# Modulation vectors of a transformer stack: one PSUM bank per group of weight slots, rows copied and turned once per group

## The chip, the cores and the metric

One Trainium2 chip, one core of it. The metric is the device time of one launch in microseconds; the kernel before took 2061.79 us (median of 3 runs, 2061.45 to 2061.92).

## The reference, cut to what matters

The kernel computes two blocks of two layers each, on 256 context tokens and 256 latent tokens of width 1024, later 16 + 256 tokens. The change concerns the modulation of the first block alone. For each of its two layers one vector for the latent tokens and one for the context tokens is made from a condition vector, and cut into six parts of 1024 numbers each (shift, scale and gate, twice):

```python
mod_lat = (silu_c @ ada_w[i] + ada_b[i])[:, None, :]
mod_ctx = (silu_cc @ ada_w[i] + ada_b[i])[None, None, :]
sh1, sc1, g1, sh2, sc2, g2 = jnp.split(mod_lat, 6, axis=-1)
...
h_lat = modulate(rmsnorm(x, norm_g[i, 0]), sh1, sc1)
...
x = x + g1 * rmsnorm(y_lat, norm_g[i, 1])
h = modulate(rmsnorm(x, norm_g[i, 2]), sh2, sc2)
x = x + g2 * rmsnorm(conv_ffn(h, ...), norm_g[i, 3])
```

`ada_w[i]` is 1024 by 6144, so both layers hold 48 pieces ("slots") of 1024 by 256, 1 MB each. The two vectors (latent and context) are multiplied together, as two columns of one small operand.

## The kernel before, in words

**Streams.** All activations lie with features on the 128 partitions. Every projection streams its weights in slots of 1 MB: SyncE loads `w_raw`, ScalarE writes `w_hi` (the rounded part), VectorE `w_lo` (the rest), and TensorE makes three products for each (lines 456 to 458, or 451 to 453). A projection of width 512 tokens has 16 steps (j) to a slot of 48 matmuls. The order of all work on an engine is the order in which the program is written; engines wait for each other by semaphores. A `fill` or `after` function puts other work between the steps or slots of a projection.

**The modulation.** A slot's product (`pe_ada_products`, matmuls on line 570) is written as rows: the stationary operand is `cvec[:, k, :]`, 32 columns of which two hold the condition vectors and 30 are zero, and the moving operand is a block of 256 columns of the slot. The eight k are spread over four groups of 32 partitions of the bank `wk[:, 2]`, two k in each, so the result is four partial sums of two rows by 256. ScalarE copies them to `ada_rows` (line 580), and two matmuls on line 593 (`pe_ada_columns`) turn them into columns and add the four parts at the same time: `ada_rows` is the stationary operand (128 by 128), and two columns of `pad` with ones in the rows 32 q and 32 q + 1 are the moving one. The result is written to `wk[:, 3]`, from which VectorE takes whole parts (`dve_mod`, line 641).

**Where the slots stand.** Eight slots are in the opening, in four pairs on two banks (`pe_ada_first`). The other 40 (g = 0 to 39) come through a ring of two buffers, `ada_ring`; ScalarE issues the load of slot g + 2 behind the copy of slot g (line 583). Slots 0 to 5 stand between the steps of the first projections, 6 to 11 in `hyb_out`, 12 to 20 around the first residual (`pe_residual`, lines 990 and 993) and the second norm (`pe_norm`, line 730: squares are summed over partitions, and slots 16, 17 and 18 stand behind the chunks c = 1, 3 and 5), 21 to 30 in the first half of the feed-forward layer, and 31 to 39 around the second residual and the third norm, as 12 to 20. In these two stretches ScalarE squares X (line 743), takes the roots (lines 999 and 747) and writes the modulated values (line 757), and VectorE takes the reciprocals (lines 1005 and 765) and updates X (line 1011). In what follows they are called the first and the second norm stretch.

**Waits.** TensorE's products of slot g wait for the ring's load of g and for ScalarE's copy of slot g - 1, because both use one bank. Its columns of slot g - 1 stand behind the products of slot g. ScalarE's copy of slot g waits for the columns of slot g - 1, because there is one buffer for the rows, and so does everything behind it on ScalarE, the load of slot g + 2 too.

## Time and profile before

| | |
|---|---|
| median of 3 runs | 2061.79 us (2061.45 to 2061.92) |
| span of the profiled execution | 2060.0 us, core clock 0.979 on average |
| own time of the profiled execution | not given apart; the runs lie 1.5 to 1.9 us above its span |
| TensorE matmul busy | 1965.3 us (95%) |
| VectorE, ScalarE, GpSimd busy | 1250.8, 934.2 and 217.6 us |
| TensorE's share of the chain that ended last | 85% |
| data moved | 296.79 MB, 144 GB/s on average |

The span is the time from the first to the last instruction of one profiled execution. Busy shares say how long an engine had work in hand; the chain that ended last says which work the end had to wait for. PEclk in a table of windows is the granted clock of TensorE as a share of 2.4 GHz.

### The profile page before, as it was taken

How to read it: one execution, taken by the hardware profiler on the slowest of the kernel's cores; microseconds unless marked ns; L12 is line 12 of the kernel's file. 1: busy time of each engine (PE TensorE's matmuls, PEld its weight loads, DVE VectorE, ACT ScalarE, POOL GpSimd, SP SyncE). 2: the span in 40 equal slices, each digit the busy share in tenths (PEclk: the TensorE clock that was granted, in tenths of full speed). 3: DMA queues.
4: the chain of work that ended last, by engine and by line, in shares of the span. 5: the costliest groups of instructions: out<-in, count | busy, mean ns of one | idle time of the engine just before them, and what ended most of it. 6: DMA issues, size and time to landing. Idle time of an engine off the chain costs nothing.

```text
span 2060.0 us, 33586 instructions
## 1 busy us (share of the span) xinstructions
PE 1965.3 (95%) x13381; PEld 1743.3 (85%) x13381; DVE 1250.8 (61%) x1853; ACT 934.2 (45%) x1477; POOL 217.6 (11%) x171
## 2 busy tenths in 40 slices
PE   5999989999999899999989998999999999989998
PEld 3776647778888579999979997998899999879997
DVE  5354455543555445667577677656975557787564
ACT  4344335332333343148455455346654444565353
POOL 2100103440452000012000000000010010000001
PEclk8999989999999999999989999999999999999999
DMA  8621464433222523222435543542345554224553
GB/s 351 221 82 62 146 243 143 164 132 118 88 89 85 204 82 123 83 103 83 143 130 172 188 166 130 184 164 79 127 164 177 171 177 143 101 90 167 186 182 123
DMA packets 43952, 296.79 MB, mean 144 GB/s; under 512 B 4976, under 2 KB 6128, under 8 KB 11696
## 3 DMA queue, kind: packets, MB, share of 16 engines
q1 hardware_dynamic: 36576, 247.48, 34.8%
q10 hardware_dynamic: 6048, 42.49, 5.9%
q0 software_dynamic: 1200, 5.02, 0.7%
q8 instruction: 91, 1.49, 0.3%
q14 instruction: 37, 0.30, 0.0%
HBM read 293.93 MB, written 1.05 MB: 143 GB/s over the span
## 4 chain that ended last, share of the span: by engine, by line
PE 85%; DVE 7%; ACT 4%; DMA 2%; issue 1%; POOL 1%; SPq 0%; ACTq 0%; DVEq 0%; POOLq 0%
PE acc L456 23%; PE acc L458 22%; PE acc L457 22%; PE acc L451 2%; PE acc L452 2%; PE acc L453 2%; DVE w_lo L393 2%; PE wk L570 2%; DMA ada_first<-in_w_ada 1%; PE wk L1671 1%; PE wk L730 1%; ACT w_hi L383 1%; PE wk L593 1%; PE acc L1660 1%; PE wk L1400 1%
## 5 line engine op out<-in xcount | busy, mean ns | idle before, releaser
L456 PE MATMUL acc<-Hhi,w_hi 128*128 128x272 f32 (+2 forms) x2304 | 742.2, 322 | 26.0 <-DVE Hlo L772 9.1
L458 PE MATMUL acc<-Hhi,w_lo 128*128 128x272 f32 (+2 forms) x2304 | 719.7, 312 | 0.0
L457 PE MATMUL acc<-Hlo,w_hi 128*128 128x272 f32 (+2 forms) x2304 | 718.9, 312 | 0.0
L393 DVE TENSOR_TENSOR w_lo<-w_raw,w_hi 128x1024 fp32r<-128x1024 f32 (+2 forms) x472 | 572.1, 1251 | 181.5 <-ACT w_hi L383 179.9
L383 ACT ACTIVATE w_hi<-w_raw 128x1024 fp32r<-128x1024 f32 (+2 forms) x472 | 452.5, 1005 | 434.0 <-PE acc L458 348.1
L456 PEld LDWEIGHTS acc<-Hhi,w_hi 128*128 128x128 f32 x2304 | 439.8, 191 | 68.9 <-issue 36.0
L457 PEld LDWEIGHTS acc<-Hlo,w_hi 128*128 128x128 f32 x2304 | 440.0, 191 | 21.8
L458 PEld LDWEIGHTS acc<-Hhi,w_lo 128*128 128x128 f32 x2304 | 439.4, 191 | 22.4
L456 PE MATMUL acc<-Fhi,w_hi 128*128 128x256 f32 (+2 forms) x864 | 264.8, 307 | 2.6 <-DVE w_lo L393 1.5
L458 PE MATMUL acc<-Fhi,w_lo 128*128 128x256 f32 (+2 forms) x864 | 264.4, 306 | 0.0
L457 PE MATMUL acc<-Flo,w_hi 128*128 128x256 f32 (+2 forms) x864 | 264.1, 306 | 0.0
L456 PEld LDWEIGHTS acc<-Fhi,w_hi 128*128 128x128 f32 x864 | 163.4, 189 | 11.2 <-issue 2.2
L458 PEld LDWEIGHTS acc<-Fhi,w_lo 128*128 128x128 f32 x864 | 163.4, 189 | 7.0
L457 PEld LDWEIGHTS acc<-Flo,w_hi 128*128 128x128 f32 x864 | 163.1, 189 | 6.7
L451 PE MATMUL acc<-w_hi,Hhi 128*128 128x256 f32 x320 | 93.2, 291 | 0.0
L1046 ACT ACTIVATE cgu<-acc,vec 128x512 f32<-128x512 f32 x44 | 34.2, 779 | 127.1 <-PE acc L458 127.1
L452 PE MATMUL acc<-w_lo,Hhi 128*128 128x256 f32 x320 | 90.4, 283 | 0.0
L453 PE MATMUL acc<-w_hi,Hlo 128*128 128x256 f32 x320 | 90.4, 283 | 0.0
L1068 DVE SCALAR_TENSOR_TENSOR cgu<-acc,vec,cgu 128x510 f32<-128x510 f32 x44 | 32.7, 745 | 92.0 <-ACT cgu L1046 92.0
L957 DVE COPY Y<-acc 128x256 f32 (+3 forms) x32 | 17.9, 558 | 81.0 <-PE acc L458 81.0
L1905 DVE TENSOR_TENSOR X<-acc,X 128x272 f32<-128x272 f32 (+3 forms) x48 | 20.4, 434 | 73.6 <-PE acc L458 73.6
L451 PEld LDWEIGHTS acc<-w_hi,Hhi 128*128 128x128 f32 x320 | 61.2, 191 | 3.2 <-issue 3.0
(390 smaller groups left out, 2452.4 us busy)
## 6 DMA issues: line engine op xcount, KB each, us to landing
w_raw<-in_w_ffn_in SPq DMA_DIRECT2D x44, 1024.0 KB, 4.9
ada_ring<-in_w_ada ACTq DMA_DIRECT2D x40, 1024.0 KB, 4.9
w_raw<-in_w_mlp_in SPq DMA_DIRECT2D x32, 1024.0 KB, 4.9
w_raw<-in_w_mlp_out SPq DMA_DIRECT2D x32, 1024.0 KB, 4.9
w_raw<-in_w_ffn_out SPq DMA_DIRECT2D x32, 704.0 KB, 4.1
ada_first<-in_w_ada SPq DMA_DIRECT2D x8, 1024.0 KB, 17.9
w_raw<-in_w_ret_v SPq DMA_DIRECT2D x8, 1024.0 KB, 4.8
w_raw<-in_w_ret_g SPq DMA_DIRECT2D x8, 1024.0 KB, 4.9
```

The costliest lines, as they stand in the source:

```text
L383: act.activation(w_hi[:, r, a:b], w_raw[:, r, a:b], ACT.Copy).then_inc(hi_done, 1)
L393: dve.tensor_tensor(w_lo[:, r, a:b], w_raw[:, r, a:b], w_hi[:, r, a:b].bitcast(F32), ALU.subtract).then_inc(lo_done, 1)
L451: pe.matmul(o, x_hi(k)[:, toks], w_hi[:, r, w], start=k == 0, stop=False)
L452: pe.matmul(o, x_hi(k)[:, toks], w_lo[:, r, w], start=False, stop=False)
L453: mm = pe.matmul(o, x_lo(k)[:, toks], w_hi[:, r, w], start=False, stop=k == last)
L456: pe.matmul(o, w_hi[:, r, w], x_hi(k), start=k == 0, stop=False)
L457: pe.matmul(o, w_hi[:, r, w], x_lo(k), start=False, stop=False)
L458: mm = pe.matmul(o, w_lo[:, r, w], x_hi(k), start=False, stop=k == last)
L570: mm = pe.matmul(wk[b:b + 32, ada_bank(s), 0:256], cvec[:, k, :], w[:, k * 256:(k + 1) * 256], start=k < 4, stop=k >= 4)
L593: mm = pe.matmul(wk[:, 3, 2 * m:2 * m + 2], ada_rows_of(s)[:, c * P:(c + 1) * P], V("pad", 0, 2), start=True, stop=True)
L1046: act.activation(cgu[:, r, c, 0:n], acc_tile(p, r, c), ACT.Identity, bias=Vd("conv_b", m + layer * 44), scale=Vd("conv_w", m + (layer * 3 ...
L1068: dve.scalar_tensor_tensor(seqs(o, 1, SEQ), seqs(acc_tile(p, r, c), 0, SEQ - 1), w, seqs(o, 1, SEQ), ALU.mult, ALU.add).then_inc(conv_left, 1)
```

## The change

Nine groups of slots take the place of 48 single ones: the four pairs of the opening, and the slots 0 to 5, 6 to 11, 12 to 20, 21 to 30 and 31 to 39 of the ring.

- The slots of a group accumulate in one bank. Slot j of a group uses a window of the stationary operand `cvec` that is shifted by 2 j columns, so its two rows land in the rows 2 j and 2 j + 1 of each 32, and all other rows get zero added. `cvec` is now 62 columns wide, and the condition vectors stand in columns 30 and 31.
- Only the first slot of a group waits for a copy (of the group before). ScalarE copies once for each group, with the last slot; for the others it only waits for the products and issues the load of slot g + 2.
- The rows are turned once for each group (`pe_ada_close`, two matmuls with 2 w moving columns for w slots, from `pad`, which now holds four identities of 32 by 32). A close is added in the feed-forward layer, behind its slot 0, for the group 12 to 20.
- `cvec` takes the memory of `rope_c`, so `rope_c` is loaded later, in `load_second` on GpSimd's queue, and the late constants are nine loads in place of ten. VectorE's memset of `cvec` has 496 elements a partition in place of 256, and `vec` has 27 columns more.

```diff
-        ("lru_lam", 8), ("subln", 1), ("lambda", 256), ("if_bias", 2), ("eps", 1), ("pad", 5),
+        ("lru_lam", 8), ("subln", 1), ("lambda", 256), ("if_bias", 2), ("eps", 1), ("pad", 32),
...
+        cvec = at("cvec", [P, DC, 62], at_const[0])
         rope_c = const("rope_c", [P, 2, T2])
...
-        ADA_READ = {ADA_LATE: 8, 0: 4, ADA_HYB: 5, ADA_OUT: 6}
+        ADA_GROUPS = [(0, ADA_HYB, 4), (ADA_HYB, ADA_OUT, 5), (ADA_OUT, ADA_FFN, 6), (ADA_FFN, ADA_LATE, 6), (ADA_LATE, ADA_RING, 8)]
+        ADA_PAIRS = ADA_FIRST // 2
...
-            if ada_back(s) > 0:
-                pe.wait_ge(ada_staged, ada_back(s))
+        def ada_products(pe, w, j, bank, first, last):
+
             for k in range(DC):
                 b = 32 * (k % 4)
-                mm = pe.matmul(wk[b:b + 32, ada_bank(s), 0:256], cvec[:, k, :], w[:, k * 256:(k + 1) * 256],
-                               start=k < 4, stop=k >= 4)
+                mm = pe.matmul(wk[b:b + 32, bank, 0:256], cvec[:, k, 30 - 2 * j:62 - 2 * j], w[:, k * 256:(k + 1) * 256],
+                               start=first and k < 4, stop=last and k >= 4)
             mm.then_inc(ada_used, 1)
 
+        def act_ada_pair(act, i):
+            act.wait_ge(ada_used, 2 * i + 2)
+            if i >= 2:
+                act.wait_ge(ada_done, i - 1)
+            act.activation(ada_rows[0][:, i % 2, :], wk[:, 1 + i % 2, 0:256], ACT.Copy).then_inc(ada_staged, 1)
+
         def act_ada(act, first, last):
 
             for s in range(first, last):
+                n, a, b, _ = ada_group(s - ADA_FIRST)
                 act.wait_ge(ada_used, s + 1)
-                if ada_back(s) > 0:
-                    act.wait_ge(ada_done, ada_back(s))
-                act.activation(ada_rows_of(s), wk[:, ada_bank(s), 0:256], ACT.Copy).then_inc(ada_staged, 1)
-                if ADA_FIRST <= s < 2 * ADA_SLOTS - 2:
+                if s - ADA_FIRST == b - 1:
+                    if n >= 1:
+                        act.wait_ge(ada_done, ADA_PAIRS + n)
+                    act.activation(ada_rows[1][:, 0, :], wk[:, 2, 0:256], ACT.Copy).then_inc(ada_staged, 1)
+                if s < 2 * ADA_SLOTS - 2:
                     g = s + 2 - ADA_FIRST
                     act.dma_start(ada_ring[:, g % 2, :], t["w_ada"][s + 2]).then_inc(ada_ring_loaded[g % 2], 16)
...
+        def pe_ada(pe, g):
+
+            n, a, b, _ = ada_group(g)
+            pe.wait_ge(ada_ring_loaded[g % 2], 16 * (g // 2 + 1))
+            if g == ADA_HYB:
+                pe.wait_ge(at_pt, 32)
+            if g == a:
+                pe.wait_ge(ada_staged, ADA_PAIRS + n)
+            ada_products(pe, ada_ring[:, g % 2, :], g - a, 2, g == a, g == b - 1)
+
+        def pe_ada_close(pe, g):
+
+            n, a, b, read = ada_group(g - 1)
+            pe.wait_ge(ada_staged, ADA_PAIRS + n + 1)
+            pe.wait_ge(s_mod, read)
+            x, w = 4 * (ADA_FIRST + a), b - a
             for c in range(2):
-                m = 2 * ada_slot(s) + c
-                mm = pe.matmul(wk[:, 3, 2 * m:2 * m + 2], ada_rows_of(s)[:, c * P:(c + 1) * P], V("pad", 0, 2),
+                o = wk[:, 3, x:x + 4 * w].rearrange("p (j x) -> p j x", x=4)[:, :, 2 * c:2 * c + 2]
+                mm = pe.matmul(o, ada_rows[1][:, 0, c * P:(c + 1) * P], V("pad", 0, 2 * w).rearrange("p (j s) -> p j s", s=2),
                                start=True, stop=True)
             mm.then_inc(ada_done, 1)
...
-            act_ada(act, 6, 8)
+            act_ada_pair(act, 3)
             hi(2)
             hi(3)
...
+            pool.dma_start(rope_c[:, :, :], t["rope_c"]).then_inc(s_meta, 16)
...
             def slots(s):
+                if s == 0:
+                    pe_ada_close(pe, ADA_FFN)
                 if ADA_FFN + s < ADA_LATE:
                     pe_ada(pe, ADA_FFN + s)
```

**TensorE in the feed-forward layer.** Between two slots of the projection, TensorE had a slot's products (line 570) and the columns of the slot before (line 593):

```order
L458 MATMUL acc<-Hhi_66,w_lo 128x512
L570 MATMUL wk<-ada_ring,cvec 32x256 x8
L593 MATMUL wk<-vec,ada_rows_89 128x2 x2
L456 MATMUL acc<-Hhi_66,w_hi 128x512
L457 MATMUL acc<-Hlo_69,w_hi 128x512
```

In the changed kernel the same place (products are now line 550) reads:

```order
L458 MATMUL acc<-Hhi_67,w_lo 128x512
L550 MATMUL wk<-ada_ring,cvec 32x256 x8
L456 MATMUL acc<-Hhi_67,w_hi 128x512
L457 MATMUL acc<-Hlo_70,w_hi 128x512
L458 MATMUL acc<-Hhi_67,w_lo 128x512
```

The two matmuls on `ada_rows` have gone; the products stand where they stood.

**TensorE at the start of the first norm stretch.** Before, from the last step of `hyb_out` over slots 12 and 13, the residual's sums (990, 993), slots 14 and 15, to the first two chunks of the norm (730):

```order
L458 MATMUL acc<-SGhi,w_lo 128x512
L570 MATMUL wk<-ada_ring,cvec 32x256 x16
L593 MATMUL wk<-vec,ada_rows_89 128x2 x2
L990 MATMUL wk<-sq_acc,ones 128x512
L993 MATMUL wk<-sq,ones 128x512 x2
L570 MATMUL wk<-ada_ring,cvec 32x256 x8
L593 MATMUL wk<-vec,ada_rows_89 128x2 x2
L570 MATMUL wk<-ada_ring,cvec 32x256 x8
L593 MATMUL wk<-vec,ada_rows_89 128x2 x2
L730 MATMUL wk<-sq,ones 128x512 x2
```

And now (the residual's sums are lines 991 and 994):

```order
L458 MATMUL acc<-SGhi,w_lo 128x512
L550 MATMUL wk<-ada_ring,cvec 32x256 x16
L991 MATMUL wk<-sq_acc,ones 128x512
L994 MATMUL wk<-sq,ones 128x512 x2
L550 MATMUL wk<-ada_ring,cvec 32x256 x16
L730 MATMUL wk<-sq,ones 128x512 x2
L550 MATMUL wk<-ada_ring,cvec 32x256 x8
```

Three pairs of column matmuls between `hyb_out` and the norm have gone, and nothing has come in; behind each later pair of norm chunks one more is gone.

**ScalarE at the end of the first norm stretch.** Before, from the last two squares to the first modulated value (line 757); line 580 is the copy of a slot, line 583 the ring's load:

```order
L743 ACTIVATE sq<-X 128x512 x2
L580 ACTIVATE ada_rows_89<-wk 128x256
L583 DMA ada_ring<-in_w_ada 128x2048
L747 ACTIVATE root<-wk,vec 128x512
L580 ACTIVATE ada_rows_89<-wk 128x256
L583 DMA ada_ring<-in_w_ada 128x2048
L580 ACTIVATE ada_rows_89<-wk 128x256
L583 DMA ada_ring<-in_w_ada 128x2048
L757 ACTIVATE n_78<-nt,mod,gains 128x256 x2
```

And now (the copy of a group is line 568, the ring's load line 571):

```order
L743 ACTIVATE sq<-X 128x512 x2
L571 DMA ada_ring<-in_w_ada 128x2048
L747 ACTIVATE root<-wk,vec 128x512
L571 DMA ada_ring<-in_w_ada 128x2048
L568 ACTIVATE ada_rows_90<-wk 128x256
L571 DMA ada_ring<-in_w_ada 128x2048
L757 ACTIVATE n_79<-nt,mod,gains 128x256 x2
```

Two of the three copies have gone, with their waits for TensorE's columns; one stays, that of the whole group with slot 20, ahead of the first modulated value.

## Rows read from the trace of the kernel before

**Rows 1.** The page's part 4: shares of the chain that ended last.

```profile
PE 85%; DVE 7%; ACT 4%; DMA 2%; issue 1%; POOL 1%; SPq 0%; ACTq 0%; DVEq 0%; POOLq 0%
```

**Rows 2.** Busy us by stretch, summed over 46:108, 220:271 and 308:460.

```profile
sum 265.00, PE 264.11 PEld 205.45 DVE 126.20 ACT 98.73 POOL 80.77; mean PE 88.04 PEld 68.48 DVE 42.07 ACT 32.91 POOL 26.92
```

**Rows 3.** One source line, L593: duration ns min/median/max, first and last start.

```profile
L593 PE MATMUL wk<-vec,ada_rows x192: 165/251/374, 22.4 to 724.1; 128*128 128x2 f32 x192
```

**Rows 4.** Timeline, TensorE, 226 to 236: start us, us, engine, line, idle before.

```profile
226.78 0.39 PE L458 MATMUL acc<-SGhi,w_lo 128*128 128x512 f32 x1
227.09 1.07 PE L570 MATMUL wk<-ada_ring,cvec 128*32 128x256 f32 x16
...
228.91 0.40 PE L456 MATMUL acc<-AThi,w_hi 128*128 128x512 f32 x1
...
232.80 0.39 PE L458 MATMUL acc<-SGhi,w_lo 128*128 128x512 f32 x1
...
234.12 0.61 PE L593 MATMUL wk<-vec,ada_rows 128*128 128x2 f32 x4
...
235.37 0.39 PE L456 MATMUL acc<-SGhi,w_hi 128*128 128x512 f32 x1
```

**Rows 5.** The chain in order of time, 272 to 306: start us, us, what.

```profile
273.28 0.28 ACT ada_rows L580
...
274.77 0.54 PE wk L593 x4
...
276.27 1.73 PE wk L993 x4
...
278.03 0.70 ACT root L999
...
289.99 1.82 PE wk L730 x4
...
296.83 4.80 DMA ada_ring<-in_w_ada
...
305.10 1.10 ACT n L757 x2
```

**Rows 6.** Timeline, 273 to 303: start us, us, engine, line, idle before.

```profile
273.70 1.07 PE L570 MATMUL wk<-ada_ring,cvec 128*32 128x256 f32 x16 [1.33 <-ACT ada_rows L580]
...
302.68 1.29 DVE L777 TENSOR_TENSOR nt<-X,rstd 128x512 f32<-128x512 f32 x2
```

**Rows 7.** Timeline, 690 to 724: start us, us, engine, line, idle before it.

```profile
690.13 1.07 PE L570 MATMUL wk<-ada_ring,cvec 128*32 128x256 f32 x16 [0.81 <-ACT ada_rows L580]
...
694.45 0.69 ACT L999 ACTIVATE root<-wk,vec 128x512 f32<-128x512 f32 x1 [0.94 <-PE wk L993]
...
698.90 1.94 PE L570 MATMUL wk<-ada_ring,cvec 128*32 128x256 f32 x16 [2.95 <-DMA ada_ring<-in_w_ada]
...
699.84 0.88 DVE L1011 SCALAR_TENSOR_TENSOR X<-nt,gains,X 128x256 f32<-128x256 f32 x2
...
701.36 0.87 DVE L1011 SCALAR_TENSOR_TENSOR X<-nt,gains,X 128x256 f32<-128x256 f32 x2
...
701.88 0.38 ACT L580 ACTIVATE ada_rows<-wk 128x256 f32<-128x256 f32 x1 [5.45 <-PE wk L593]
...
717.52 0.69 ACT L747 ACTIVATE root<-wk,vec 128x512 f32<-128x512 f32 x1 [1.38 <-PE wk L730]
...
723.24 1.08 ACT L757 ACTIVATE n<-nt,mod,gains 128x256 f32<-128x256 f32 x2
```

**Rows 8.** One source line, L583: the ring's transfers, issue to landing.

```profile
DMA to landing us min/median/max: 4.7/4.9/7.2
```

**Rows 9.** Busy us of each engine and PEclk in stretches of 2 us.

```profile
273.00:275.00 2.00, 1.30 (x19) 0.80 (x19) 0.00 (x0) 0.56 (x2) 0.00 (x0) 1.00 0.78 201
...
285.00:287.00 2.00, 1.99 (x3) 0.91 (x4) 1.97 (x6) 0.63 (x1) 0.00 (x0) 0.50 0.65 274
```

**Rows 10.** Timeline, ScalarE, around 37.

```profile
37.13 0.38 ACT L580 ACTIVATE ada_rows<-wk 128x256 f32<-128x256 f32 x1 [1.32 <-PE wk L570]
```

More of the change, by code:

```diff
@@ L470, in stack_kernel @@
         CONSTS2 = [("ident", ident), ("one_row", one_row), ("sgu_w", sgu_w), ("sgu_b", sgu_b), ("dist", dist),
-                   ("rope_ret", rope_ret), ("head_sel", head_sel), ("swap_ret", swap_ret), ("swap_c", swap_c),
-                   ("rope_c", rope_c)]
+                   ("rope_ret", rope_ret), ("head_sel", head_sel), ("swap_ret", swap_ret), ("swap_c", swap_c)]
         N_CONST, N_CONST2, N_BIAS = 16 * len(CONSTS), 16 * len(CONSTS2), 16
@@ L548, in ada_back, with ada_group @@
-        def ada_back(s):
-            return s - 1 if s < ADA_FIRST else s
-        def pe_ada_products(pe, s):
-            if s < ADA_FIRST:
-                w = ada_first[s][:, :]
-                if s == 0:
-                    pe.wait_ge(s_cvec, 1)
-                if s % 2 == 0:
-                    pe.wait_ge(ada_loaded[s // 2], 2 * 16)
-            else:
-                g = s - ADA_FIRST
-                w = ada_ring[:, g % 2, :]
-                pe.wait_ge(ada_ring_loaded[g % 2], 16 * (g // 2 + 1))
-                if g == ADA_HYB:
-                    pe.wait_ge(at_pt, 32)
-            if ada_back(s) > 0:
-                pe.wait_ge(ada_staged, ada_back(s))
+        def ada_group(g):
+            n = next(i for i, (a, b, _) in enumerate(ADA_GROUPS) if a <= g < b)
+            return n, *ADA_GROUPS[n]
@@ L582, in act_ada, with pe_ada_first @@
+                if s < 2 * ADA_SLOTS - 2:
                     g = s + 2 - ADA_FIRST
                     act.dma_start(ada_ring[:, g % 2, :], t["w_ada"][s + 2]).then_inc(ada_ring_loaded[g % 2], 16)
-        def pe_ada_columns(pe, s):
-            pe.wait_ge(ada_staged, s + 1)
-            if s - ADA_FIRST in ADA_READ:
-                pe.wait_ge(s_mod, ADA_READ[s - ADA_FIRST])
-            if s < ADA_FIRST and s % 2 == 0 and s > 0:
-                pe.wait_ge(s_mod, s // 2)
+        def pe_ada_first(pe):
+            pe.wait_ge(s_cvec, 1)
+            for i in range(ADA_PAIRS):
+                pe.wait_ge(ada_loaded[i], 2 * 16)
+                if i >= 2:
+                    pe.wait_ge(ada_staged, i - 1)
+                for j in range(2):
+                    ada_products(pe, ada_first[2 * i + j][:, :], j, 1 + i % 2, j == 0, j == 1)
+                pe.wait_ge(ada_staged, i + 1)
+                if i >= 1:
+                    pe.wait_ge(s_mod, i)
+                for c in range(2):
+                    o = wk[:, 3, 0:32].rearrange("p (j x) -> p j x", j=2)[:, :, 4 * i + 2 * c:4 * i + 2 * c + 2]
+                    mm = pe.matmul(o, ada_rows[0][:, i % 2, c * P:(c + 1) * P],
+                                   V("pad", 0, 4).rearrange("p (j s) -> p j s", s=2), start=True, stop=True)
+                mm.then_inc(ada_done, 1)
@@ L591, in pe_ada_columns @@
             for c in range(2):
-                m = 2 * ada_slot(s) + c
-                mm = pe.matmul(wk[:, 3, 2 * m:2 * m + 2], ada_rows_of(s)[:, c * P:(c + 1) * P], V("pad", 0, 2),
+                o = wk[:, 3, x:x + 4 * w].rearrange("p (j x) -> p j x", x=4)[:, :, 2 * c:2 * c + 2]
+                mm = pe.matmul(o, ada_rows[1][:, 0, c * P:(c + 1) * P], V("pad", 0, 2 * w).rearrange("p (j s) -> p j s", s=2),
                                start=True, stop=True)
             mm.then_inc(ada_done, 1)
-        def pe_ada_first(pe):
-            for i in range(ADA_FIRST // 2):
-                for s in (2 * i, 2 * i + 1):
-                    pe_ada_products(pe, s)
-                for s in (2 * i, 2 * i + 1):
-                    pe_ada_columns(pe, s)
@@ L604, in pe_ada @@
-        def pe_ada(pe, g):
-            pe_ada_products(pe, ADA_FIRST + g)
-            if g not in ADA_READ:
-                pe_ada_columns(pe, ADA_FIRST + g - 1)
-        def pe_ada_close(pe, g):
-            pe_ada_columns(pe, ADA_FIRST + g - 1)
         def act_out_scaled(act, name, j):
@@ L3061, in _packed @@
     put("eps", np.full((P, 1), EPS, np.float32))
-    rows = np.zeros((P, 2), np.float32)
-    for j in range(4):
-        rows[32 * j, 0] = rows[32 * j + 1, 1] = 1.0
-    put("pad", rows)
+    put("pad", np.tile(np.eye(32, dtype=np.float32), (4, 1)))
     return cols
```

24 lines of the change are left out of this document (10 added, 14 removed).

## The prediction

> **What bounds the kernel now.** I read the chain that ended last first: 85% of it lies on TensorE [rows 1], so what the change saves elsewhere counts only where TensorE waits for it. Then the busy time by stretch. In the three stretches where the ring's slots 0 to 11 and 21 to 30 stand between dense projections, TensorE is busy 264.11 of 265 us [rows 2]: whatever is taken from TensorE there is taken from the time. The rest of the modulation stands in the opening and in the two norm stretches (271 to 308 and 690 to 726), where the three engines take turns. There I followed the chain in order of time [rows 5] and the timeline [rows 6, 7]: TensorE, ScalarE and the ring's loads are all on it. Behind 730 us nothing changes but one load that nobody waits for.
>
> **The price of one pair of column matmuls.** The source line has 192 matmul records for 48 slots, so four to a slot [rows 3]. A slot's products alone take 2.13 us from the last projection matmul before them to the fourth behind them (226.78 to 228.91); with columns the same distance is 2.57 us (232.80 to 235.37), with L593 starting at 234.12 [rows 4]. So one pair costs 0.44 us of TensorE's time, weight loads included. I take that from the spacing, not from the 0.54 that the chain gives to such a piece [rows 5], because that holds a drain which the next matmul overlaps.
>
> **Dense stretches.** Columns stood there with slots 1 to 5 (the close for 0 to 5 stays), 7 to 11 (its close stays too) and 21 to 30 (ten, and a close). Now 21 to 30 have the new close behind slot 0 of the feed-forward layer and the old one at the end, so nine go. 5 + 5 + 9 = 19 pairs, 19 x 0.44 = **8.4 us**.
>
> The closes have up to 20 moving columns in place of 2. Below that costs nothing; above, a 512-column pair on L993 takes 1.73 us for two matmuls [rows 5], 0.87 each, so 20 columns are at most 0.03 us by proportion, 0.3 us for all ten that close ring groups. I take nothing: the first row's 2 columns already show a price that is not in proportion to the columns. The Trainium skill, TensorEngine Tiling (Array Packing), section Instruction Overhead, says that a matmul with one moved column takes as long as one with sixty; no row here has twenty, and the sum would be the same by it.
>
> **First norm stretch.** Step by step, before against now.
> - Slot 13's products waited 1.33 us for the copy of slot 12 [rows 6], because both used the bank; that copy is gone. So are the columns of slot 12 (0.44) ahead of the residual's sums. Root L999 at 278.03 [rows 5] comes at 276.2: **-1.8**. The last square on which L993 waits is done where the copy began, at 273.28, as early as the sums now start, so it doesn't hold them.
> - Three pairs of columns stood between the norm's sums (behind the chunks 1, 3 and 5), on TensorE's way to root L747: 3 x 0.44 = **-1.3**. X is updated every 1.52 us by VectorE (699.84 to 701.36 in the second stretch [rows 7]). TensorE needed 1.82 for two sums [rows 5] and 1.44 for a slot; now 2.82 for two chunks against VectorE's 3.04, but VectorE was ahead by two chunks and shifts by 1.8 as well, so TensorE still ends last.
> - The modulated values started at 305.10 [rows 5], while their input `nt` was written from 302.68 on, two in 1.29 us [rows 6], the first at 303.33. ScalarE was held by the copies of slots 19 and 20: the ring's load of slot 20 left at 296.83, took 4.80, and products, columns and copy filled the 3.5 us behind it. Now this load leaves when slot 18's products end, at 293.5 (296.83 less 1.8, less 2 x 0.44 for the columns before it, less some 0.6 for its own columns and the start of the copy); it lands at 298.4, the products take 1.07 or 1.94 by the clock [rows 4, 7], the group's copy 0.4, so ScalarE is free between 299.8 and 300.7. The input is ready at 303.33 - 3.1 = 300.2. Start between 300.2 and 300.7: **-4.4 in all** for this stretch, 4.3 to 4.9.
>
> **Second norm stretch.** The same program with other waits.
> - Slot 32's products waited 0.81 for a copy [rows 7]; with its columns that gives root L999 at 694.45 - 1.3 = 693.2.
> - X's first chunk was ready at 700.7 (699.84 + 0.88), but ScalarE sat 5.45 us until 701.88 for columns, because slot 34's load landed only at 698.90 [rows 7]. It squared X at 702.3. That load now leaves at 690.4 in place of 691.9; with 4.9 to 7.2 us to land [rows 8] it is there at 695.3 to 697.6, and its products are done by 699.5 even at the low clock. X is ready at 700.7 - 1.3 = 699.4. **-2.9**.
> - Three pairs between the sums, -1.3, less 0.3 for a new wait: stepping on from 699.4 with 1.82 or twice that for two sums and 1.0 or 1.9 for a slot, slot 37's load leaves with slot 35's products at 705.3 and lands at 710.4, and TensorE gets there at 710.1. Root L747 717.52 - 3.9 = 713.6.
> - Slot 39's load leaves at 711.5, lands at 716.4, products until 717.5 to 718.3, copy 0.4. The modulated values start at 718.0 to 718.7 in place of 723.24 [rows 7]: **-4.8 in all**, 4.5 to 5.2.
>
> **The rest.** In the opening eight copies become four and four column pairs go. Its end hangs on the last pair of slots: the last copy starts at 37.13 behind TensorE [rows 10], and ScalarE's next work behind it. The copy of a pair starts behind the same matmul, so nothing is gained; bound from below, had the copy itself been on the way, 0.4. I take 0. The memset's 240 more elements and 14 KB more of `vec` lie under the first loads. `rope_c` is one load less in the late constants, and one more on GpSimd's queue in `load_second`, where the value is used hundreds of us later; without that cover it would cost one load, at most the ring's 7.2 us [rows 8], and that takes a landing hundreds of us late. ScalarE's 39 copies of 0.38 us [rows 7] are hidden behind its waits for TensorE, except where counted.
>
> The new waits: the first slot of a group waits for the group's copy before, which stands a whole slot of a projection earlier each time. The close of slots 12 to 20 waits for a copy that ends before the projection starts.
>
> Sum: 8.4 + 4.4 + 4.8 = 17.6. The profiled span of 2060.0 goes to 2042.4; the median of the runs shown lies 1.8 above the span, so **2044.2 us**. Bounds of the terms: 8.0 to 8.6, 4.3 to 4.9, 4.5 to 5.2, opening 0 to 0.4: 2042.7 to 2045.0, and with 1 us for what a shifted program does to its loads 2041.7 to 2046.5.
>
> **The rivals.**
> - *The ring's loads become the bound.* In the norm stretches two slots now take 5.64 us on TensorE (2 x 2.82), and one ring buffer needs a landing of 4.9 plus 1.0 for the products, 5.9 [rows 8]. I counted this as 0.3. If the loads, sooner on one another's heels, take up to the 7.2 seen, each stretch loses twice 2.2 (slots 18 and 20, 37 and 39), at worst all but the first root's gain. With half of it, 4.4, the time is 2048.6; with all, 2053. For it: one load did take 7 us. Against: half of them took 4.7 to 4.9. Chance 0.15.
> - *TensorE's clock.* It was 1.00 in 273 to 275, across the idle 1.33 us [rows 6, 9], and 0.50 in 285 to 287 [rows 9], behind TensorE's wait for the first square of X; slot 34's products took 1.94 us in place of 1.07 behind an idle 2.95 [rows 7]. The change takes work off TensorE in just these stretches, and the idle piece ahead of the first sum grows by 0.6 us in the first stretch by my times, while others shrink. If the clock stayed at the low of its two levels (1.2 GHz) over what ran at the high one, each stretch's L993 (1.73), three pairs of sums (1.82) and five slots of 1.00 [rows 4, 5] would double: 12.2 a stretch, 24.4 in all, 2068.6, slower than before. It decides once 17.6 of the 24.4 is slow. Against: an idle of 1.33 us left the clock high, and between those sums my times hold none above 0.3. Chance 0.02. The Trainium skill, TensorE: Matmul & The Clock Gate, section HAM oscillation, says that an array which waits between bursts is throttled and starts each burst cold; that speaks against this change, and by it the first two sums of each stretch stay slow as they are now, which the sum above already holds.
> - *The clock does better.* In the second stretch the idle piece ahead of slot 34 shrinks from 2.95 us to 2 or none; if the clock holds, slot 34 takes 0.9 less and the first two sums 1.8 less: 2.7 at most, and X's pace bounds it to about 1.5 of that, 3.7 us less for the very best case of both stretches. 2042.7 down to 2040.5. Chance 0.08.
> - *The change does not do what it says for time*: the dense stretches give 8.4, but ScalarE's order makes new waits that eat the norm stretches' gain, 2053.4, or more. Chance 0.05, of which 0.02 for under 4 us of gain in all.
>
> **How the numbers follow.** The forecast has 0.70. Its own range is 2041.7 to 2046.5. To hold 8 in 10 I add the better clock and the nearer half of the first rival: 2041 to 2050. 0.2% is 4.1 us, about what a measurement of this kernel can tell from no change. Slower: 0.02 for the clock and 0.01 for an unseen wait; within 0.2%: 0.03; faster 0.94.
>
> **What would show it.** Column matmuls fall from 192 records to 36. In the dense stretches a slot between projections should cost 2.13 us each time. Slot 13's products should stand right behind slot 12's. From root L999 (then L1000) to the first modulated value it was 27.1 us in the first stretch and 28.8 in the second [rows 5, 7]; it should be 24.5 and 25.3. PEclk should read 1.00 between the sums of chunks 2 to 7. A ring wait over 1 us at slots 17 to 18 or 36 to 37 would speak for the first rival, a PEclk of 0.50 there for the second.

## The result and the profile after

The changed kernel took 2050.59 us (median of 4 runs, 2049.29 to 2051.30) against 2061.68 for the kernel before on the same chip: ratio 0.9944, 95% interval 0.9933 to 0.9956. So it gained 11.1 us where the prediction had 17.6. Faster, as forecast; the time lies 6.4 us above the forecast and 0.6 above the range. The profiled execution has a span of 2049.6 us where it was 2060.0. Most of this gap turns out to lie in work that the change doesn't touch.

The share of the chain that ended last (part 4 of the page) still says TensorE [rows 1]:

```profile
PE 83%; DVE 8%; ACT 4%; DMA 2%; issue 1%; POOL 1%; SPq 0%; DVEq 0%; ACTq 0%; POOLq 0%
```

The column matmuls, by source line (duration ns min/median/max, first and last start), are 16 + 20 = 36 records in place of 192 [rows 3]:

```profile
L587 PE MATMUL wk<-vec,ada_rows x16: 244/253/273, 24.1 to 38.0; 128*128 128x4 f32 x16
...
L609 PE MATMUL wk<-vec,ada_rows x20: 176/262/285, 101.9 to 712.5; 128*128 128x12 f32 x8, 128*128 128x18 f32 x8, 128*128 128x20 f32 x4
```

The records with 12 to 20 moved columns have a median of 262 ns, those with 2 had 251 [rows 3]: the closes cost next to nothing more. TensorE's timeline in `hyb_out` (start us, us, engine, line) shows two slots' products between projection matmuls, both without columns now:

```profile
225.47 0.40 PE L458 MATMUL acc<-SGhi,w_lo 128*128 128x512 f32 x1
225.80 1.07 PE L550 MATMUL wk<-ada_ring,cvec 128*32 128x256 f32 x16
...
227.61 0.40 PE L456 MATMUL acc<-AThi,w_hi 128*128 128x512 f32 x1
...
231.57 0.40 PE L458 MATMUL acc<-SGhi,w_lo 128*128 128x512 f32 x1
231.90 1.07 PE L550 MATMUL wk<-ada_ring,cvec 128*32 128x256 f32 x16
...
233.71 0.39 PE L456 MATMUL acc<-SGhi,w_hi 128*128 128x512 f32 x1
```

The distance is 2.14 us both times (227.61 - 225.47, 233.71 - 231.57). Before it was 2.13 without columns and 2.57 with them [rows 4]: the price of 0.44 was right. In the first half of the feed-forward layer two slots with products between them fell from 7.12 to 6.70 us, 0.42 each.

**What nobody looked for.** In the second half of the feed-forward layer (`ffn0_out0` and `ffn0_out1`, 16 slots of 33 matmuls of 512 columns on `Fhi` and `Flo`), where the diff changes nothing, VectorE's copies of Y out of the accumulators mark the slots. Of the kernel before:

```profile
455.81 0.69 DVE L957 COPY Y<-acc 128x512 f32 x1 [2.29 <-PE acc L458]
463.30 0.69 DVE L957 COPY Y<-acc 128x512 f32 x1 [5.02 <-PE acc L458]
470.78 0.69 DVE L957 COPY Y<-acc 128x512 f32 x1 [5.01 <-PE acc L458]
478.26 0.69 DVE L957 COPY Y<-acc 128x512 f32 x1 [5.01 <-PE acc L458]
```

And of the changed kernel:

```profile
446.73 0.69 DVE L958 COPY Y<-acc 128x512 f32 x1 [2.29 <-PE acc L458]
454.43 0.69 DVE L958 COPY Y<-acc 128x512 f32 x1 [5.24 <-PE acc L458]
462.13 0.69 DVE L958 COPY Y<-acc 128x512 f32 x1 [5.24 <-PE acc L458]
469.83 0.69 DVE L958 COPY Y<-acc 128x512 f32 x1 [5.24 <-PE acc L458]
```

A slot went from 7.48 to 7.70 us, at a clock of 1.00 in both, and VectorE waits for TensorE alone: 16 x 0.22 = 3.5 us lost. The same kind of matmul stands in `hyb_out`, on `AThi` and `SGhi`: there a slot with products fell from 7.12 to 6.80 us, 0.32 where 0.44 was due. Across its six slots that makes some 0.7, so 4.2 us in all. What does the change have to do with it? `pad` in the constants' block grew from 5 to 32 columns, so every tile laid out behind that block, these operands too, moved by 96 bytes (27 columns of 4 bytes; places are multiples of 32).

**The first norm stretch** gained 2.8 us in place of 4.4. Its timeline of TensorE, ScalarE and its queue (ACTq issues the ring's loads):

```profile
268.46 1.93 PE L550 MATMUL wk<-ada_ring,cvec 128*32 128x256 f32 x32
...
269.60 0.33 ACTq L571 DMA_DIRECT2D ada_ring<-in_w_ada  x1
...
270.46 0.69 ACTq L571 DMA_DIRECT2D ada_ring<-in_w_ada  x1
...
273.20 0.69 ACT L1000 ACTIVATE root<-wk,vec 128x512 f32<-128x512 f32 x1 [0.74 <-PE wk L994]
...
275.51 1.49 PE L550 MATMUL wk<-ada_ring,cvec 128*32 128x256 f32 x16 [2.35 <-DMA ada_ring<-in_w_ada]
...
278.25 1.93 PE L550 MATMUL wk<-ada_ring,cvec 128*32 128x256 f32 x16 [1.25 <-DMA ada_ring<-in_w_ada]
...
280.63 1.15 ACT L743 ACTIVATE sq<-X 128x512 f32<-128x512 f32 x2 [6.74 <-PE wk L550]
...
281.31 3.78 PE L730 MATMUL wk<-sq,ones 128*128 128x512 f32 x4 [1.13 <-ACT sq L743]
...
299.39 1.09 ACT L757 ACTIVATE n<-nt,mod,gains 128x256 f32<-128x256 f32 x2 [0.38 <-DVE nt L777]
```

Slots 12 and 13 run back to back (`x32`), as forecast, and the root comes at 273.20. But the loads of slots 14 and 15, issued behind them, now leave 0.86 us apart. They land after 5.9 and 7.8 us (the products at 275.51 and 278.25 start with them) against a median of 4.9 [rows 8]; TensorE idles 2.35 and 1.25 us, and ScalarE, which waits for slot 15's products, squares X only at 280.63, though VectorE had it ready at 279.46 (6.26 us behind the root). Slot 15's products take 1.93 us in place of 1.07 and the first sums of two chunks 3.78: the granted clock is at 0.50. (These sums were slow before too, 3.45 us.) From the root to the first modulated value it is 26.19 us; 24.5 was forecast. The second stretch came out as said: root at 687.03, value at 712.38, so 25.35 where 25.3 was forecast; the experiments show how much of that was luck.

### The profile page after: what moved, and what is told of

It is laid out like the page before. It is cut to its first block, busy times and chain, and to the rows that moved or that the text cites. A ratio compares the mean times of both kernels' runs of the same rounds, so it can differ in the third digit from the quotient of the medians.

```text
span 2049.6 us, 33160 instructions
## 1 busy us (share of the span) xinstructions
PE 1947.9 (95%) x13225; PEld 1720.8 (84%) x13225; DVE 1251.7 (61%) x1853; ACT 920.7 (45%) x1438; POOL 217.4 (11%) x171
## 4 chain that ended last, share of the span: by engine, by line
PE 83%; DVE 8%; ACT 4%; DMA 2%; issue 1%; POOL 1%; SPq 0%; DVEq 0%; ACTq 0%; POOLq 0%
PE acc L456 23%; PE acc L458 22%; PE acc L457 22%; DVE w_lo L393 2%; PE acc L451 2%; PE acc L453 2%; PE acc L452 2%; PE wk L550 2%; DMA ada_first<-in_w_ada 1%; PE wk L1672 1%; PE wk L730 1%; ACT w_hi L383 1%; PE acc L1661 1%; PE wk L1401 1%; DMA ada_ring<-in_w_ada 1%
## 5 line engine op out<-in xcount | busy, mean ns | idle before, releaser
L456 PEld LDWEIGHTS acc<-Fhi,w_hi 128*128 128x128 f32 x864 | 162.2, 188 | 12.4 <-issue 2.2
L976 ACT ACTIVATE sq<-Y 128x512 f32<-128x512 f32 (+1 forms) x32 | 16.4, 523 | 122.1 <-DVE Y L958 61.9
## 6 DMA issues: line engine op xcount, KB each, us to landing
ada_first<-in_w_ada SPq DMA_DIRECT2D x8, 1024.0 KB, 18.3
```

The lines of the kernel that those rows point to most:

```text
L456: pe.matmul(o, w_hi[:, r, w], x_hi(k), start=k == 0, stop=False)
```

## The experiments

Every kernel is compared with the kernel before on its own chip, whose median was 2061.76, 2062.65, 2062.51 and 2062.07 us in the four sets (e, f, g, h). "Block moved by n" means bytes by which the tiles behind the constants lie further than in the kernel before. "Root to n" is from the residual's root to the first modulated value (`n`) in the first and the second stretch, written as a sum: from the root to ScalarE's first square of X, and from there to n. The last four columns are from one traced execution of each run.

| run | block moved | time us | slot of `ffn0_out` | slot of `hyb_out` | root to n, 1st | root to n, 2nd |
|---|---|---|---|---|---|---|
| before | 0 | 2061.68 | 7.48 | 7.12 | 6.29 + 20.78 = 27.07 | 7.83 + 20.96 = 28.79 |
| after | 96 | 2050.59 | 7.70 | 6.80 | 7.43 + 18.76 = 26.19 | 6.30 + 19.05 = 25.35 |
| e1_after_aligned | 128 | 2049.35 | 7.67 | 6.79 | 7.27 + 18.93 = 26.20 | 6.61 + 19.22 = 25.83 |
| e2_before_pad32 | 96 | 2064.86 | 7.70 | 7.25 | 6.30 + 20.84 = 27.14 | 6.60 + 20.64 = 27.24 |
| e3_before_pad21 | 64 | 2060.54 | 7.55 | 7.15 | 6.30 + 20.93 = 27.23 | 6.58 + 20.53 = 27.11 |
| e4_small_loads | 128 | 2047.34 | 7.67, 7.70 | 6.79 | 6.30 + 18.43 = 24.73 | 6.29 + 18.72 = 25.01 |
| f1_after_256 | 256 | 2048.61 | 7.48 | 6.70 | 6.82 + 19.33 = 26.15 | 7.35 + 18.29 = 25.64 |
| f2_before_256 | 256 | 2062.36 | 7.48 | 7.13 | 6.29 + 20.85 = 27.14 | 7.19 + 20.99 = 28.18 |
| f3_opening_undone | 256 | 2047.04 | 7.48 | 6.70 | 6.29 + 18.17 = 24.46 | 8.23 + 19.34 = 27.57 |
| f4_slot15_later | 256 | 2045.95 | 7.48 | 6.70 | 6.29 + 17.99 = 24.28 | 6.69 + 19.11 = 25.80 |
| g1_operands_moved | 128 | 2046.93 | 7.48 | 6.79 | 6.30 + 19.23 = 25.53 | 7.81 + 18.41 = 26.22 |
| g2_both_priced_out | 256 | 2047.19 | 7.48 | 6.70 | 6.30 + 19.13 = 25.43 | 6.29 + 19.65 = 25.94 |
| g3_slot15_again | 256 | 2047.99 | 7.48 | 6.70 | 6.30 + 18.44 = 24.74 | 8.28 + 19.24 = 27.52 |
| g4_after_again | 96 | 2050.09 | 7.70 | 6.80 | 6.30 + 18.70 = 25.00 | 6.29 + 19.06 = 25.35 |
| h1_fillers | 256 | 2045.26 | 7.48 | 6.70 | 6.90 + 16.97 = 23.87 | 6.38 + 18.64 = 25.02 |
| h2_fillers_slot15 | 256 | 2045.13 | 7.48 | 6.70 | 6.29 + 17.24 = 23.53 | 8.17 + 19.34 = 27.51 |
| h3_after_256_again | 256 | 2049.26 | 7.48 | 6.70 | 6.30 + 19.23 = 25.53 | 7.56 + 18.41 = 25.97 |

### Is it the place of the tiles?

```diff
--- e1_after_aligned (on the changed kernel)
-        ... ("eps", 1), ("pad", 32),
+        ... ("eps", 1), ("pad", 40),
--- e2_before_pad32, e3_before_pad21 (on the kernel before)
-        ... ("eps", 1), ("pad", 5),
+        ... ("eps", 1), ("pad", 32),        (21 in e3)
```

> The changed kernel with pad 8 columns wider still (972 columns of vec), so that all tensors behind the constants start at the same place modulo 64 bytes as in the kernel before; in the changed kernel they start 32 bytes past such a boundary. Theory (address): the 512-column matmuls of the feed-forward output projections go back from 0.2333 to 0.2267 us apart, a slot there from 7.70 to 7.48 us, 16 slots give 3.5 us, hyb_out another 0.6: 2046.5 us. Rival (the slower slots come from the accumulation, from the ring's loads or from the moved rope_c load): nothing changes, 2050.6 us, slots at 7.70.

> The kernel before with pad 32 columns wide in place of 5 and nothing else: everything behind the constants moves by 96 bytes, to 32 past a multiple of 64. Theory (address): a slot of the output projections goes from 7.48 to 7.70 us, the time from 2061.7 to 2065.8 us. Rival: 2061.7 us, slots at 7.48.

> The kernel before with pad 21 columns wide: the same move by 64 bytes, a multiple of 64 but not of 128. If the boundary that counts is 64 bytes: 2061.7 us, slots at 7.48. If it is 128 bytes, or any move costs: about 2065.8 us, slots at 7.70.

The kernel before with nothing but 27 more columns in `pad` has the slots of 7.70 us and is slower, ratio 1.0017 (1.0008 to 1.0026): the move alone does it, not the accumulation in one bank. But a move of 128 bytes, a multiple of 64, stayed at 7.67, so a rule of 64 bytes falls. The kernel before moved by 64 bytes hit neither of its two figures either: 7.55, a third of the 0.22, and a time that can't be told from the kernel before, ratio 0.9997 (0.9987 to 1.0006). The next pair asked whether 256 does it.

```diff
--- f1_after_256 (on e1_after_aligned)
-        ... ("pad", 40),
+        ... ("pad", 72),
--- f2_before_256 (on the kernel before)
-        ... ("pad", 5),
+        ... ("pad", 69),
```

> The changed kernel with everything behind the vector block moved so that it lies 256 bytes behind its place in the kernel before. Theory (where Fhi, Flo, AThi and SGhi lie within 256 bytes sets how fast the matmuls on them are issued): slots of ffn0_out0 and ffn0_out1 back at 7.48 us as in the kernel before (7.70 in the changed kernel, 7.67 with 128 bytes), those of hyb_out at 6.68 instead of 6.80; 16 x 0.19 + 6 x 0.1 = 3.6 us less than the 2049.35 of 128 bytes, 2045.8 us. Rival (any move of the block costs this, or the place within 256 bytes is not what counts): slots stay at 7.67 to 7.70 and the time at 2049.3 us.

> The kernel before with the same move of 256 bytes and nothing else. Theory: slots of 7.48 us and the time of the kernel before, 2061.8 us. Rival: slots of 7.6 to 7.7 us and 2064.5 us, as with 96 bytes (2064.86 us).

Both have their 7.48 us back, and f2 the time of the kernel before, ratio 0.9999 (0.9990 to 1.0008). The total of f1, however, fell by 0.7 us only, not by 3.6: its slots gave 3.6 and something later took 2.5 away (below). Which tile is it? g1 takes e1, slots of 7.67, and moves only the feed-forward operands and their scratch on:

```diff
-        F_hi = {T1: at("Fhi512", [P, FFH, T1], A + 16 * KB, F32R), ...
+        F_hi = {T1: at("Fhi512", [P, FFH, T1], A + 16 * KB + 128, F32R), ...
-        F_lo = {T1: at("Flo512", [P, FFH, T1], A + 38 * KB, F32R), ...
+        F_lo = {T1: at("Flo512", [P, FFH, T1], A + 38 * KB + 128, F32R), ...
-        cgu = at("cgu", [P, 2, 2, T1], A + 60 * KB)
+        cgu = at("cgu", [P, 2, 2, T1], A + 60 * KB + 128)
...
```

> The run e1_after_aligned (block moved by 128 bytes) with the tiles of ffn0's output matmuls, Fhi and Flo for 512 tokens, and their scratch put 128 bytes further, so that they lie where they lie with a move of 256 bytes; all else stays. Theory (the place of the operand that a matmul streams counts): the 16 slots of ffn0_out0 and ffn0_out1 take 7.48 us instead of 7.67, those of hyb_out stay at 6.79; 3.0 us less than e1_after_aligned, 2046.3 us. Rival (it is another tile or the weights whose place counts): 7.67 us and 2049.3 us.

The copies of Y in g1_operands_moved (VectorE's timeline) are 7.47 to 7.49 apart again, while `hyb_out`, whose operands stayed, kept its 6.79:

```profile
445.59 0.69 DVE L958 COPY Y<-acc 128x512 f32 x1 [2.28 <-PE acc L458]
453.08 0.69 DVE L958 COPY Y<-acc 128x512 f32 x1 [5.03 <-PE acc L458]
460.56 0.69 DVE L958 COPY Y<-acc 128x512 f32 x1 [5.01 <-PE acc L458]
```

Each against the kernel before on its own chip, e1 was 12.4 us faster and g1 15.6: 3.2 us for moving five tiles by 128 bytes. (The changed kernel on g1's chip, g4, was 12.4 faster, as e1.) So the matmul's pace depends on where its own streamed operand lies, with the weights, their tiles and everything else in place. `cgu`, `sg` and `hid` moved along, but no matmul here reads them.

### What made the first norm stretch longer than forecast?

First the loads: e4 leaves all but 128 of 2,048 columns of the slots 14, 15, 33 and 34 unloaded (their modulation is then computed from old data).

```diff
--- e4_small_loads (on e1_after_aligned)
-                    act.dma_start(ada_ring[:, g % 2, :], t["w_ada"][s + 2])...
+                    n_load = 128 if g in (14, 15, 33, 34) else SLOT
+                    act.dma_start(ada_ring[:, g % 2, 0:n_load], t["w_ada"][s + 2][:, 0:n_load])...
```

> As the first kernel (aligned), but the ring's loads of slots 14, 15, 33 and 34 bring 128 columns in place of 2048, so the modulation is not that of the reference. Theory (two loads issued 0.86 us apart share the transfer engines, land after 5.9 and 7.8 us, and hold TensorE, its clock and ScalarE): in the first norm stretch both slots' products stand right behind the residual's sums, ScalarE squares X as soon as it is there (1.1 us earlier), the first modulated value comes 1 to 2 us earlier against the residual's root; second stretch 0 to 1 earlier; 1.5 to 2.5 us in all below the first kernel, 2044.5 us. Rival (the clock or VectorE sets this part whatever the loads do): within 0.5 us of the first kernel.

It was 2.0 us faster than e1, and the stretch 1.5 shorter. That looked like the answer. But the same cut on f1 did less:

> The run f1_after_256 with the loads of slots 14, 15, 33 and 34 cut to 128 of 2,048 columns, so that both costs that the prediction left out are gone. If they are the whole miss, the time is that of the prediction, 2044.2 us, and it lies 3.3 us under e4_small_loads (2047.34) and 2.0 us or more under f1_after_256 (2048.61), whose profiled execution lost 2.5 us to a lower clock between 1,800 and 1,900 us. Rival (f1_after_256 shows that the slots' gain is given back later each time): 2046.6 us.

Measured 2047.19 us, above both figures expected and nearer to the rival's: the first stretch went from 26.15 to 25.43 only, and the prediction's 2044.2 was not reached. And the changed kernel itself, run again, needed 25.00 us with its loads in full:

> The changed kernel unaltered, for a comparison with the others on one chip: 2050.6 us, slots of 7.70 us; root to first n 26.2 us in the first norm if the late loads are there each time, down to 24.5 if they came by chance.

Its loads of slots 14 and 15 left 0.86 us apart too (268.54 and 269.41), but the products started 4.8 and 6.4 us behind them, at 273.37 and 275.82, where it had been 5.9 and 7.8. So the late loads are not the whole of it, how late they are changes from one execution to the next, and one trace is not enough here. A move of work on ScalarE's side was tried too: its wait for slot 15's products held the square of X, as the timeline above shows (6.74).

```diff
--- f4_slot15_later, g3_slot15_again (on f1_after_256)
-            act_ada(act, ADA_FIRST + ADA_OUT + 2, ADA_FIRST + ADA_OUT + 4)
+            act_ada(act, ADA_FIRST + ADA_OUT + 2, ADA_FIRST + ADA_OUT + 3)
...
-                     between=lambda c: act_ada(act, ...) if c in (3, 5, 7) else None)
+                     between=lambda c: act_ada(act, ...) if c in (1, 3, 5, 7) else None)
```

> The run f1_after_256 with ScalarE's wait for slot 15's products, and its load behind them, put between the second and the third of the first norm's squares instead of ahead of the norm. Theory (ScalarE stands behind slot 15 while X is ready for the square): the square of X starts up to 1.2 us earlier, the first root to first n falls from 26.2 to 25.0 us, and the time is 1.1 us under f1_after_256. Rival (TensorE itself waits for slot 15's load ahead of the first sums, so the squares wait for nothing that counts): within 0.2 us of f1_after_256.

> The kernel of f4_slot15_later once more, beside the changed kernel on one chip, as the best version so far: 2046 us, 4.6 us under the changed kernel (3.6 from the place of the tiles, 1 from the first norm), ratio to before 0.992. If f4_slot15_later was luck of the clock: 2048 us.

24.28 and 24.74 us in the first stretch, 1.9 and 1.4 under f1; but h3, the kernel of f1 once more, had 25.53, f3, which has the same program here as f1, 24.46, and the two totals, 2045.95 and 2047.99, differ by more than the 1.1 in question (2048 us was expected if the first was luck of the clock). The move can give back only what slot 15 holds ScalarE up, 0.5 us in f1 (6.82 against 6.29 from root to square) and nothing in h3; the rest of the difference isn't shown to be its doing.

The other thing that differs between these executions is the granted clock. Busy us of each engine, PEclk and DMA in stretches of 4 us: the changed kernel,

```profile
272.00:276.00 4.00, 1.66 (x15) 0.51 (x17) 2.01 (x1) 1.15 (x2) 0.00 (x0) 1.00 0.99 406
276.00:280.00 4.00, 2.75 (x28) 0.71 (x20) 3.93 (x6) 0.00 (x0) 0.00 (x0) 0.50 0.58 176
280.00:284.00 4.00, 2.87 (x7) 1.18 (x4) 3.93 (x9) 1.66 (x3) 0.00 (x0) 0.50 0.96 352
284.00:288.00 4.00, 4.00 (x21) 1.28 (x20) 3.90 (x9) 0.92 (x3) 0.00 (x0) 0.72 0.33 72
```

and g4, the same kernel:

```profile
272.00:276.00 4.00, 1.36 (x21) 0.57 (x24) 3.06 (x1) 0.69 (x1) 0.00 (x0) 1.00 0.98 356
276.00:280.00 4.00, 1.76 (x18) 0.56 (x10) 3.90 (x9) 0.67 (x2) 0.00 (x0) 1.00 0.93 381
280.00:284.00 4.00, 3.61 (x19) 1.10 (x18) 3.93 (x8) 1.85 (x3) 0.00 (x0) 0.57 0.27 111
284.00:288.00 4.00, 4.00 (x30) 1.58 (x23) 3.93 (x10) 1.26 (x2) 0.00 (x0) 1.00 0.65 211
```

Over the 16 us TensorE was about as idle in both, and the loads as busy, but in one the clock was at the lower level (1.2 of 2.4 GHz) for some 10 us, in the other for under 4.

The sums in the table keep two costs apart. The first is the late load of slot 15. Where it holds nothing up, ScalarE squares X 6.3 us behind the root, as soon as VectorE has it; in the changed kernel this was 7.43, in e1 7.27, in f1 6.82, each time behind slot 15's products. The second is what follows, from the square to n: 24.5 less 6.3, so 18.2 us, were forecast; without fillers it was 18.0 to 19.3. There the clock counts. In h3 slot 15 was in time and the square came 6.30 behind the root, but the first sums and slot 16's products ran at the lower clock (273.45 and 275.92 are the slots 14 and 15):

```profile
273.45 1.07 PE L550 MATMUL wk<-ada_ring,cvec 128*32 128x256 f32 x16 [1.59 <-DMA ada_ring<-in_w_ada]
275.92 1.07 PE L550 MATMUL wk<-ada_ring,cvec 128*32 128x256 f32 x16 [1.39 <-DMA ada_ring<-in_w_ada]
...
278.87 3.78 PE L730 MATMUL wk<-sq,ones 128*128 128x512 f32 x4 [1.89 <-ACT sq L743]
282.58 1.94 PE L550 MATMUL wk<-ada_ring,cvec 128*32 128x256 f32 x16
```

It needed 19.23 us from the square to n. In f3, with first sums of 3.65 us, slot 16's products took 1.07 again, and it needed 18.17: by windows of 1 us its clock was low for about as long as h3's, 7 us, but from 276 to 282 and so more of it over the wait, where h3's was from 278 to 284. Nor is a late load needed for the clock to fall: in g2, which hardly loads the slots 14 and 15, TensorE waits for the square itself.

```profile
277.61 3.78 PE L731 MATMUL wk<-sq,ones 128*128 128x512 f32 x4 [5.15 <-ACT sq L744]
281.32 1.94 PE L550 MATMUL wk<-ada_ring,cvec 128*32 128x256 f32 x16
```

The last set put the clock to the test: matmuls that nobody reads fill TensorE's waits, and the loads stay as they are.

```diff
--- h1_fillers (on f1_after_256; h2_fillers_slot15: the same on f4_slot15_later)
             for g in (2, 3):
+                for i in range(4 if g == 2 else 1):
+                    pe.matmul(wk[:, 0, 0:512], ones[:, :], rope_ret[:, :, :], start=True, stop=True)
                 pe_ada(pe, ADA_OUT + g)
+            pe.matmul(wk[:, 0, 0:512], ones[:, :], rope_ret[:, :, :], start=True, stop=True)
             pe_norm(pe, 1, ...
```

> The run f1_after_256 with six matmuls that nobody reads (ones on rope_ret, 512 columns, into the bank of the norm's sums before these start): four ahead of slot 14's products, one ahead of slot 15's and one ahead of the first sum of the first norm. Theory (what makes this stretch long is TensorE's clock, which falls to 0.50 while TensorE waits for the two late loads and stays there for 6 to 10 us): the granted clock stays at 1.00 until the first sums, and the first root to the first n takes 24.7 us or less where f1_after_256 took 26.15; 1.2 us less in all. Rival (the loads set the stretch and the clock only goes with them): 25.5 to 26.2 us, and the time of f1_after_256 or 0.3 us above it.

> The kernel of f4_slot15_later with the same six matmuls. Theory of the clock: 24.0 us from the first root to the first n (24.28 and 24.74 without them), and 2046 us, the lowest of all. Rival: no lower than f4_slot15_later, 2046 to 2048 us.

> The kernel of f1_after_256 once more, beside the two with the matmuls. If its 26.15 us from the first root to the first n and the 0.93 of clock between 1,800 and 1,900 us are its own: both again, and 2048.6 us. If they are chance from one execution to the next: 24.7 to 25.5 us, 0.98, and 2047 us.

The same windows of h1:

```profile
272.00:276.00 4.00, 4.00 (x21) 1.64 (x23) 3.12 (x1) 0.69 (x1) 0.00 (x0) 1.00 0.77 326
276.00:280.00 4.00, 3.92 (x33) 1.31 (x23) 3.90 (x9) 0.73 (x2) 0.00 (x0) 1.00 0.64 201
280.00:284.00 4.00, 4.00 (x23) 1.31 (x22) 3.93 (x9) 1.79 (x3) 0.00 (x0) 1.00 0.90 326
284.00:288.00 4.00, 3.63 (x22) 1.09 (x20) 3.93 (x10) 1.76 (x3) 0.00 (x0) 1.00 0.90 299
```

and TensorE's timeline there:

```profile
271.89 3.60 PE L2995 MATMUL wk<-rope_ret,ones 128*128 128x512 f32 x8
275.42 1.07 PE L550 MATMUL wk<-ada_ring,cvec 128*32 128x256 f32 x16
276.42 1.13 PE L2995 MATMUL wk<-rope_ret,ones 128*128 128x512 f32 x2
277.47 1.07 PE L550 MATMUL wk<-ada_ring,cvec 128*32 128x256 f32 x16
278.47 1.12 PE L2997 MATMUL wk<-rope_ret,ones 128*128 128x512 f32 x2
279.67 2.04 PE L730 MATMUL wk<-sq,ones 128*128 128x512 f32 x4
```

The clock stays at 1.00 in all four windows; slots 14 and 15 take 1.07 each and the first sums 2.04. Root to n is 23.87 us in h1 and 23.53 in h2, against 25.53 in h3 on the same chip and 26.15 in f1. It doesn't come from earlier loads: slot 15's products started 5.4 us behind the root in h1 and 5.05 in the changed kernel, and the square came at 6.90. The gain lies behind it, 16.97 us from the square to n in h1 and 17.24 in h2, where no execution without fillers had under 17.99. So by these traces the lower clock costs this stretch 1.8 to 2.4 us in the changed kernel, e1, f1 and h3, and 1.2 in f3. Not all of that is part of the miss, since the forecast had left the first sums as slow as they were before. By the Trainium skill, TensorE: Matmul & The Clock Gate, section HAM oscillation, an array that keeps waiting for its data is throttled again and starts each burst cold. The first sums agree with it, 3.78 us in h3 behind its waits and 2.04 in h1 with the waits filled; the products of slots 14 and 15 in h3 and g4, 1.07 us each behind waits of 1.25 to 1.59, do not. h1 took 2045.26 us (2043.85 to 2046.33) and h3 2049.26 (2047.98 to 2049.82), 4.0 us between medians, of which the stretch explains 1.7 to 2.3.

Much of the rest, in the two traces, is another drop of the clock, far behind. PEclk between 1,800 and 1,850 us is 0.86 in h3_after_256_again and 0.97 in h1_fillers:

```profile
1800.00:1850.00 50.00, 44.95 (x285) 38.43 (x282) 38.59 (x69) 27.10 (x68) 0.00 (x0) 0.86 0.32 107
```

```profile
1800.00:1850.00 50.00, 40.97 (x284) 35.22 (x283) 40.85 (x70) 31.45 (x79) 3.95 (x5) 0.97 0.37 127
```

From the next norm's first modulated value, near 1,037 us in f1, to the end of the span f1, g2 and h3 need 1009.4 to 1009.7 us; the other fourteen traces of this study, of the old program and the new, need 1005.1 to 1007.2. That is where f1 lost its 2.5 us, twice with the same kernel. What brings it on, while the program there is the same in f3, f4, g3, h1 and h2, stays open; f3, f4 and g3 go without it and without fillers, so nothing shows that the fillers keep it away.

### Does the opening cost something?

The first acc matmul to slot 0's products took 27.4 us before and 28.1 after, with the clock rising later in the opening. f3 undoes the opening alone (own banks, one copy and two column pairs for each slot).

```diff
--- f3_opening_undone (on f1_after_256), excerpt
-                for j in range(2):
-                    ada_products(pe, ada_first[2 * i + j][:, :], j, 1 + i % 2, j == 0, j == 1)
+                for s in (2 * i, 2 * i + 1):
+                    ...
+                    ada_products(pe, ada_first[s][:, :], 0, 2 - s % 2, True, True)
```

> The run f1_after_256 with the opening's eight slots as in the kernel before (own banks, a copy and two pairs of columns each), the ring's slots in groups. Theory (less work on TensorE in the opening lets its clock rise later): first acc matmul to slot 0's products 27.3 us instead of 28.1, and 0.8 us less than f1_after_256. Rival (the later clock is chance, the opening's change costs and gives nothing): within 0.2 us of f1_after_256.

The distance was 28.2 us with the opening undone and 27.1 in f1 with the opening of the changed kernel, the opposite of what my theory said. The changed kernel once more (g4) had 27.1, and the kernel before moved by 256 bytes (f2) 28.5: the 0.7 us is chance of the clock, not of the change. f3's lower total comes from the norm stretch and from the clock behind 1,800 us, neither of which it touches.

## Why the prediction was wrong

- *One pair costs 0.44, 19 pairs 8.4 us*: right. 2.14 against 2.13 between matmuls, and with its operands back in place `hyb_out` went from 7.12 to 6.70 a slot.
- *Closes, copies and the opening at nothing*: right; 20 moved columns cost 0.01 us more than 2 by the median record, and f3 finds no price for the opening.
- *"1 us for what a shifted program does to its loads"*: **this is the step that failed.** I had counted that `vec` grows by 27 columns and priced only its load ("14 KB more of `vec` lie under the first loads"). What it moved was not asked. 16 slots by 0.22 and six of `hyb_out` by about 0.1: 4.2 us of the 6.4 by the slots; the medians of e1 and g1 show 3.2 of it for the 16 slots alone. The same sentence has its bound wrong by its own terms: 2045.0 and 1 are 2046.0, not 2046.5.
- *First norm stretch, -4.4*: the first root's part was right (from the last slots of `hyb_out` to the root 1.9 us less, 1.8 forecast). Mis-sized is the rest: root to n 26.19 in place of 24.5, so 1.7 us. I had slots 14 and 15 in time. Their loads left 0.86 us apart, and slot 15's products held ScalarE's square of X up, 7.43 us behind the root in place of 6.29: 1.1 us. The other 0.6 came behind the square (18.76 in place of 18.2), where the clock was low for the first sums and part of slot 16's products. The rival on the loads asked about the wrong ones (slots 18 and 20); the rival on the clock asked whether it stays low through the whole stretch. What came was between them. The size is that of one execution: in the seven traces with the changed program here (after, e1, f1, f3, g1, g4, h3) root to n was 24.46 to 26.20, on average 25.6, 1.1 above the forecast.
- *Second norm stretch, -4.8*: 28.79 to 25.35 and a root 1.3 earlier as forecast, but one of its two parts was luck. I had said that ScalarE would no longer sit behind slot 34's load (7.83 us from root to square, 1.5 of it waiting). In the changed kernel's trace it came at 6.30. But in f3, g3 and h2 it came at 8.2 to 8.3, behind slot 34's products again, and that is 1.9 of the 2.2 us by which they exceed the changed kernel's 25.35; the mean is 7.05 over the four traces of the old program and 7.10 over the thirteen of the new one (7.24 without e4 and g2, where this load is cut). So this wait comes and goes with the execution, and the change didn't remove it. The other part stands: from the square to n the old program took 20.5 to 21.0 us, the new one 18.3 to 19.7, 1.8 less on average. That is what the change is worth between root and n, not 3.4. I had read the waits of one execution as the kernel's.
- *The sum*: 17.6 - 4.2 - 1.7 = 11.7, and the 0.7 of the opening's clock takes it to 11.0. In the two traces the second stretch's first n comes 10.9 us earlier (723.24 and 712.38), the spans differ by 10.4, the medians by 11.1.

Of the versions tried, h1_fillers (operands back in their place within 256 bytes, TensorE's waits filled) is the fastest together with h2: ratio 0.9919 (0.9906 to 0.9933) to the kernel before, and 0.9918 for h2_fillers_slot15, the same within what can be told.

## What to carry to other kernels

A change that resizes a constant moves every tile behind it. Compare first the stretches that the diff does not touch, slot by slot; if a dense matmul there has another pace at the same clock, pad the block until its streamed operands lie where they lay. And where engines take turns, two executions of one kernel differ by more than a us in one stretch: price a wait there from several traces, split at the first instruction that the wait can hold up, and treat TensorE's idle gap as dearer than its length, since the clock may fall in it and stay low for some us of real work; a few matmuls without a reader can be cheaper.
